# A hybrid decoder step: retention decay as factors, the causal mask added on TensorE, the ffn norm weights held in SBUF

## The chip, the cores and the metric

One of the eight cores of a Trainium2 chip runs the whole kernel; the others idle. The metric is the time of the kernel on the device in microseconds (us), the median of several executions.

## What is computed

One layer of a hybrid decoder in float32, for a prompt of 1024 tokens and for 8 sequences of 4 new tokens each (32 rows). The reference, cut to what matters here:

```python
def attend(q, k, v, q_pos, k_pos):                      # 8 heads of 96 (64 + 32 rotary)
    s = einsum('...qhd,...khd->...hqk', q, k) * 96 ** -0.5
    s = where(k_pos[None, :] <= q_pos[:, None], s, -inf)     # causal mask
    return einsum('...hqk,...khd->...qhd', softmax(s), v)

def retention_chunk(R, qkv):                            # chunks of 128 tokens, 8 heads of 64
    q, k, v = qkv
    lg = log1p(-2.0 ** (-5.0 - arange(8)))              # log decay of each head
    dmat = where(i >= j, exp(lg * (i - j)), 0.0)
    o = einsum('bhij,bjhv->bihv', einsum('bihd,bjhd->bhij', q, k) * dmat, v)
    o = o + einsum('bihd,bhdv->bihv', q, R) * exp(lg * (i + 1))
    R_new = exp(lg * 128) * R + einsum('bjhd,bjhv->bhdv', k * exp(lg * (127 - j)), v)
    return R_new, o

def peer_block(xb, ...):                                # 8 heads x 16 experts per token
    # queries against two sets of 128 keys, top 16 of each, top 16 of their 256 sums
    act = gelu(einsum('nd,nhkd->nhk', xb, peer_u[experts]))
    return einsum('nhk,nhkd->nd', softmax(vs) * act, peer_v[experts])

h = x + concat([mla_out, silu(rg) * group_norm(o)]) @ w_o
y = h + peer(rms_norm(h, ffn_norm_w))
```

The experts' tables `peer_u` and `peer_v` have 16384 rows of 1024 floats each. Every token gathers 128 rows of each.

## The kernel before

The program is written out engine by engine, with explicit semaphores. The prompt is cut into 8 tiles of 128 tokens (t = 0 to 7); the 32 new tokens are tile 8 ("the sample"), whose attention work is hung into tiles 1, 2 and 3.

**A tile's front** goes through these stages: projection of the normed x by ten weight pieces of 1 MB; latents, queries, keys, values and retention; attention of 8 heads over (t + 1) x 128 keys; the output projection (4 pieces); the residual and the ffn norm; the peer queries (8 pieces), the products with the two key sets, and the top-16 searches on VectorE that give the expert numbers (`codes`) and gates. Tiles 2, 4 and 6 are hosts: their input projection also does that of the next tile, the guest, so that tiles 3, 5 and 7 load no input weights. Tiles 2 and 3 also carry half of the sample's attention over paged caches.

**The expert stream** runs beside the front of the next tile. For each of a tile's 128 slots GpSimd (POOL) issues two indirect DMAs of 128 rows (512 KB): the u rows (`u_rows`, L805) into a ring of 8 buffers and the v rows (`v_rows`, L818) into a ring of 9. VectorE takes the dot of each u row with the token (`dot`, L1775, one multiply-and-reduce of 1024 columns). After 32 dots ScalarE applies the gelu (L1345) into `gelus`, VectorE multiplies by the gates into `coefs` and transposes (`make_coefs`, L1761), ScalarE spreads the coefficients into `Z` (L1361), and TensorE adds the v rows, weighted, into PSUM (`v_round`, L863). An object `Pace` holds a list of how many slots each engine does at each point of the front; on VectorE, TensorE and ScalarE the calls `slots()` do them in program order, between the front's own work. In attention, four slots stand beside each head in tiles 4 and 6, four or five in 5 and 7, and one or two in tiles 1 to 3.

**SP** issues all other DMAs, in one written order (`front`, L633; `load_tile`, L598; `load_piece`, L613). Two 1 MB buffers `wbuf` take the weight pieces in turn; in tile 0 the idle rings serve as eight more. A piece waits until the buffer's former piece is used. Since SP waits in order, each wait holds up all loads behind it.

**The table.** One buffer `table` of 128 x 1024 floats (L220) is used for three things in turn in every tile:
- the decay matrices `dec_in` of 8 heads (128 x 128 each), loaded by `load_tile` (L609) right after x and the rotary rows. `retention_decay` (L1950) multiplies the inner products by them (`inT`);
- the causal mask, (t + 1) x 128 columns, loaded by `load_mask` (L631) once the decay has been used. `attention` on VectorE (L1974) adds it to the scores of a head, taken from PSUM, and finds their maximum in the same instruction;
- the ffn norm weights, broadcast over partitions, loaded once all heads' scores are done (L666), in tiles 2 and 3 after the sample's scaled scores (L659). `norm_ffn` (L2000) multiplies by them. In those tiles `table` is also the scratch of a root (L400).

**Retention** in `qkv_and_retention` on TensorE (L1039): `retention_turn` transposes rq and rk (scaled by 0.125 in ScalarE's copy, L1516), `retention_inner` multiplies them, then come the cross products of q with the state R (L1060) and the new state's part kd x v (L1064), both signalled by `cross_ps`. `retention_out` (L1032) multiplies the decayed inner products by v (L1035). `heads_turn` (L1005) transposes queries and keys; it waits for `R_ready` of this tile, that is for VectorE's `retention_state` (L1955), which scales the cross products into `oret` (two halves), decays R and adds the new part. `retention_sum` (L1963) adds the inner part from PSUM. `heads_turn` is followed by the first scores (L1083), each signalled to VectorE by `scores_ps`; the next head's scores wait for `scores_ready`, since there is one score buffer in PSUM.

The constants (14 small loads, L763) are issued at the start between weight piece 1 and piece 2; VectorE waits for all of them in tile 0's `project`.

## Time and profile before

| what | us |
|---|---|
| median of 3 runs | 3536.87 |
| lowest and highest of them | 3530.06, 3540.1 |
| span of the profiled execution | 3534.4 |

The profiled execution is one of its own; the page gives its span, from the first to the last instruction, and no other time of it. PE is TensorE, PEld its weight loads, DVE VectorE, ACT ScalarE, POOL GpSimd, SP the engine that issues the plain DMAs (SPq its queue). A line is one of the kernel; L1745 and L1749 are the helpers through which most of VectorE's instructions pass, so those are told apart by the tiles they name. "x16" counts instructions; "[0.72 <-DVE nb]" is the idle time before an instruction and what ended it. "Issue" as a releaser means that the trace shows nothing the engine waited for. PEclk is TensorE's granted clock as a share of 2.4 GHz. The DMA share is the mean busy share of 16 DMA engines, GB/s what they moved.

### The profile page before, as it was taken

The numbers are of one execution on the slowest core, as the hardware profiler recorded it, in microseconds if no ns is written. First come the engines' busy times: TensorE is split into PE (matmuls) and PEld (weight loads), VectorE is DVE, ScalarE is ACT, GpSimd is POOL, SyncE is SP. The second block draws the span as 40 slices with busy tenths as digits, with TensorE's granted clock in tenths as the row PEclk, the third lists the DMA queues.
The fourth block names the chain that finished last, engine by engine and source line by source line (L and its number), as shares of the span: only waits on it lengthen the run. The fifth ranks groups of instructions, "written<-read, shape, count | busy, mean of one in ns | idle before, by whom it ended". The sixth has DMA issues, their size and how long they took to land.

```text
span 3534.4 us, 35434 instructions
## 1 busy us (share of the span) xinstructions
PE 2634.4 (75%) x11810; PEld 1284.3 (36%) x11810; DVE 2374.2 (67%) x6243; ACT 433.3 (12%) x980; POOL 2393.4 (68%) x2118
## 2 busy tenths in 40 slices
PE   6658676788867798797766777797877778767656
PEld 5634123553432344362232223463332234313211
DVE  4686667667678786767478765867478766847642
ACT  1101100113101231111001110111001110000000
POOL 0155776667757776657767777657767776677876
PEclk8879779898888989899889888999888999988799
DMA  6478999999999999999999999999999999999999
GB/s 252 169 277 313 367 349 408 352 397 369 366 404 362 380 348 408 407 400 377 380 411 402 388 377 409 395 412 395 381 410 397 396 399 407 397 408 384 322 410 371
DMA packets 372025, 1321.73 MB, mean 374 GB/s; under 512 B 60674, under 2 KB 72130, under 8 KB 351618
## 3 DMA queue, kind: packets, MB, share of 16 engines
q0 software_dynamic: 304128, 1107.43, 81.0%
q1 hardware_dynamic: 67714, 212.03, 15.4%
q8 instruction: 93, 1.52, 0.2%
q14 instruction: 90, 0.74, 0.1%
HBM read 1311.41 MB, written 7.88 MB: 373 GB/s over the span
## 4 chain that ended last, share of the span: by engine, by line
POOL 26%; PE 25%; DMA 22%; DVE 15%; issue 10%; SPq 2%; ACT 1%; DVEq 0%; POOLq 0%; ACTq 0%
POOL v_ring L818 13%; POOL u_ring L805 12%; DMA v_ring<-down_rows,codesT 12%; PE ps L863 8%; PE ps L927 6%; DMA u_ring<-up_rows,codes 6%; DMA wbuf<-weights 4%; DVE u_ring L1775 3%; DVE arena L1745 3%; PE ps L917 2%; PE ps L1127 2%; PE ps L1180 2%; DVE idx L1745 1%; DVE top_c L1745 1%; DVE top_v L1745 1%
## 5 line engine op out<-in xcount | busy, mean ns | idle before, releaser
L863 PE MATMUL ps<-v_ring,Z 128*32 128x512 f32 x4096 | 1324.0, 688 | 606.6 <-DMA v_ring<-down_rows,codesT 479.3
L1775 DVE CUSTOM_DVE_ANT_0 u_ring<-u_ring,xn 128x1024 f32<-128x1024 f32 x1056 | 1260.7, 1219 | 596.0 <-DMA u_ring<-up_rows,codes 595.5
L805 POOL DMA_INDIRECT u_ring<-up_rows,codes x1056 | 1191.4, 1128 | 676.6 <-issue 305.8
L818 POOL DMA_INDIRECT v_ring<-down_rows,codesT x1056 | 1200.8, 1137 | 449.3 <-issue 297.9
L863 PEld LDWEIGHTS ps<-v_ring,Z 128*32 128x32 f32 x4096 | 242.9, 118 | 1404.0 <-DMA v_ring<-down_rows,codesT 836.4
L927 PE MATMUL ps<-wbuf,xT 128*128 128x256 f32 (+2 forms) x1184 | 287.4, 401 | 64.8 <-DMA wbuf<-weights 36.5
L1127 PEld LDWEIGHTS ps<-xT,wbuf 128*128 128x128 f32 x2176 | 269.0, 202 | 160.8 <-issue 106.8
L1127 PE MATMUL ps<-xT,wbuf 128*128 128x128 f32 (+1 forms) x2176 | 292.1, 290 | 38.9 <-DMA wbuf<-weights 38.8
L927 PEld LDWEIGHTS ps<-wbuf,xT 128*128 128x128 f32 (+1 forms) x1184 | 226.8, 198 | 139.8 <-DMA wbuf<-weights 41.1
L1745 DVE MAX8 vals<-arena 128x8 f32<-128x128 f32 (+1 forms) x288 | 69.0, 280 | 113.9 <-ACT arena L1560 113.3
L917 PE MATMUL ps<-wbuf,kT 128*128 128x256 f32 (+1 forms) x480 | 104.7, 371 | 0.0
L1083 PE MATMUL ps<-kT,qT 96*128 96x512 f32 (+3 forms) x192 | 88.3, 573 | 15.7 <-DVE nb L1749 14.1
L1522 ACT ACTIVATE arena<-arena,nb 128x128 f32<-128x128 f32 (+7 forms) x64 | 49.6, 775 | 375.1 <-DVE nb L1749 375.1
L917 PEld LDWEIGHTS ps<-wbuf,kT 128*128 128x128 f32 x480 | 88.8, 190 | 11.2
L1775 DVE DVE_READ_ACCUMULATOR2_ANT dots<- 128x1 f32 x1056 | 86.6, 82 | 0.0
L1974 DVE CUSTOM_DVE_ANT_0 arena<-ps,table 128x128 f32<-128x128 f32 (+7 forms) x64 | 48.4, 756 | 51.3 <-PE ps L1083 42.2
L1745 DVE FIND_INDEX8 idx<-vals,arena 128x8 uint32<-128x128 f32 (+1 forms) x288 | 78.3, 283 | 0.0
L1560 ACT ACTIVATE arena<-ps 128x256 f32<-128x256 f32 (+1 forms) x72 | 27.4, 381 | 413.2 <-PE ps L1137 372.3
L1101 PEld LDWEIGHTS ps<-vN,arena 128*128 128x128 f32 x576 | 72.5, 198 | 6.2 <-issue 5.9
L1101 PE MATMUL ps<-vN,arena 128*128 128x64 f32 x576 | 74.7, 276 | 0.0
L1749 DVE TENSOR_REDUCE arena<-arena 128x8 f32<-128x512 f32 (+1 forms) x72 | 49.3, 684 | 37.0 <-ACT arena L1660 35.8
L1552 ACT ACTIVATE arena<-ps 128x256 f32<-128x256 f32 (+1 forms) x72 | 26.3, 366 | 370.7 <-PE ps L1127 370.7
(332 smaller groups left out, 2358.2 us busy)
## 6 DMA issues: line engine op xcount, KB each, us to landing
wbuf<-weights SPq DMA_DIRECT2D x142, 1024.0 KB, 8.3
u_ring<-up_rows,codes POOLq DMA_INDIRECT x1056, 8.6
v_ring<-down_rows,codesT POOLq DMA_INDIRECT x1056, 8.8
u_ring<-weights SPq DMA_DIRECT2D x8, 1024.0 KB, 14.7
v_ring<-weights SPq DMA_DIRECT2D x8, 1024.0 KB, 14.9
wbuf<-weights SPq DMA_DIRECT2D x9, 768.0 KB, 7.5
resid<-x_prompt SPq DMA_DIRECT2D x8, 512.0 KB, 7.0
table<-decay_in SPq DMA_DIRECT2D x8, 512.0 KB, 10.3
```

The costliest lines, as they stand in the source:

```text
L805: pool.indirect_dma_start(out=u_ring[:, i % U_RING, :], out_offset=None, in_=up_rows, in_offset=bass.IndirectOffsetOnAxis(ap=codes[:, t % ...
L818: pool.indirect_dma_start(out=v_ring[:, v % V_RING, :], out_offset=None, in_=down_rows, in_offset=bass.IndirectOffsetOnAxis(ap=codesT[:, t ...
L863: mm = pe.matmul(acc[32 * c:32 * c + 32, half, :], (Zs if t == TILES else Z)[:, at:at + GS], v_ring[:, v % V_RING, half * 512:(half + 1) * ...
L917: mm = pe.matmul(ps[:, 2 + S_BANK[w // 2], (w % 2) * PIECE:(w % 2) * PIECE + cols], xT_of(t + 1)[:, c], weights_of(t, w)[:, c, 0:cols], st ...
L927: mm = pe.matmul(out, xT[:, c, 0:n], weights_of(t, w)[:, c, 0:cols], start=(c == 0), stop=(c == DC - 1))
L1083: mm = pe.matmul(ps[:, 2 + c // 512, 0:e - c], qT[0:QK, s, :], kT[0:QK, s, c:e], start=True, stop=True)
L1101: mm = pe.matmul(ps[:, 6, h * 64:(h + 1) * 64], probT[:, h % 2, j * P:(j + 1) * P], vN[:, j, h * 64:(h + 1) * 64], start=(j == 0), stop=(j ...
L1127: mm = pe.matmul(ps[:, 4 + s % 2, j * P:j * P + n], weights_of(t, w)[:, c, j * P:(j + 1) * P], xT[:, c, 0:n], start=(c == 0), stop=(c == D ...
L1180: pe.matmul(ps[0:n, 6 + m % 2, :], lhs, uk, start=True, stop=True).then_inc(kn_ps, 1)
L1522: own.raises(act.activation(scores[:, s % 2, 0:w], scores[:, s % 2, 0:w], ACT.Exp, bias=nb[:, s:s + 1], scale=SCALE, accum_out=sums[:, s:s ...
L1745: own.done(instruction_of(*args, **kwargs))
L1775: dve.tensor_tensor_reduce(u, u, xn[:, t % 2], 1.0, 0.0, ALU.mult, ALU.add, dots[:, k:k + 1]).then_inc(dot_done, 1)
```

## The change

- The decay exp(lg (i - j)) is taken apart. The key side uses `kd` (k times exp(lg (127 - j)) / 8), which the state needs anyway: TensorE transposes kd in place of rk, and the inner products are only multiplied by a 0/1 triangle `upto` (128 x 128, broadcast over heads). The query side, exp(lg (i + 1 - 128)), is multiplied once on the sum of inner and cross part (`dec_out`).
- For that the state R is decayed first (in VectorE's `qkv`, from tile 1 on), and the cross products are accumulated into the same PSUM region as the inner ones, in `retention_out`. TensorE waits for `kd_ready` before `retention_turn`, and for `R_ready` (2t + 1) before `retention_out`; `heads_turn` waits for it no longer. VectorE scales the two halves from PSUM and adds the new part to R in `retention_sum`.
- The mask is added on TensorE: behind a head's scores, one product identity x `causal` (128 x 128) accumulates onto the last block. VectorE's instruction keeps its form; its second operand is a column of zeros, broadcast.
- The ffn weights lie in `ffn_wb`, loaded once; `causal`, `upto` and `ffn_wb` are three more constants. To make room, gelu and coefficients are written in place in `dots`; the root's scratch in tiles 2 and 3 becomes `lat`, `latn` and `th`, for which VectorE waits for the latents' store.
- All loads of `table` go, with SP's waits before them (`inner_ready`, `scores_ready`, `sT_ready`), and the order of the other loads stays.

```diff
...
         k2T = sb("k2T", [P, P])
-        dec_cross = sb("dec_cross", [P, H])
+        dec_out = sb("dec_out", [P, H])
+        causal = sb("causal", [P, P])
+        upto = sb("upto", [P, P])
+        none = causal[:, 0:1]
         dec_k = sb("dec_k", [P, H])
...
         rope_t = sb("rope_t", [P, 192])
-        table = sb("table", [P, D])
+        ffn_wb = sb("ffn_wb", [P, D])
         wbuf = sb("wbuf", [P, 2, DC, PIECE])
...
         kpw8 = arena[:, 3744:4000]
-        root_s = (table[:, 0:288], table[:, 288:576], table[:, 576:864])
+        root_s = (lat[:, 0:288], latn[:, 0:288], th[:, 0:288])
         mla_s = qflat[0:ST, 0:512]
...
                 sp.dma_start(rope_t[:], rope_rows[t * P:(t + 1) * P, :]).then_inc(tile_in, 16)
-                sp.dma_start(table[:], decay_in).then_inc(tile_in, 16)
...
                 sp.dma_start(pe, lat[0:n, QR + KVR:LAT]).then_inc(lat_stored, 16)
-
-            def load_mask(t):
-
-                sp.wait_ge(inner_ready, in_order(t) + 1)
-                sp.dma_start(table[:, 0:(t + 1) * P], mask_rows[:, (TILES - 1 - t) * P:TILES * P]).then_inc(mask_in, 16)
...
                 store_latents(t, lat_prompt[t * P:(t + 1) * P, :], pe_prompt[t * P:(t + 1) * P, :], P)
-                load_mask(t)
                 if t == S_TILE:
...
                 load_piece(t, O_0)
-                if t == B_TILES[0]:
-                    load_piece(t, O_0 + 1)
-                if t in B_TILES:
-                    sp.wait_ge(sT_ready, B_TILES.index(t) + 1)
-                    sp.dma_start(table[:], ffn_w.partition_broadcast(P)).then_inc(ffn_in, 16)
-                if t != B_TILES[0]:
-                    load_piece(t, O_0 + 1)
+                load_piece(t, O_0 + 1)
                 if t == S_TILE:
                     store_states()
-                if t not in B_TILES:
-                    sp.wait_ge(scores_ready, H * (t + 1))
-                    sp.dma_start(table[:], ffn_w.partition_broadcast(P)).then_inc(ffn_in, 16)
                 if t == B_TILES[-1]:
...
                              (q_wb, q_w.partition_broadcast(P)), (k_wb, k_w.partition_broadcast(P)),
-                             (ret_wb, ret_w.partition_broadcast(P)), (dec_cross, decay_cross), (dec_k, decay_k),
+                             (ret_wb, ret_w.partition_broadcast(P)), (dec_out, decay_out), (dec_k, decay_k),
                              (dec_state, decay_state), (k1T, keys1T), (k2T, keys2T), (ptab, page_table),
-                             (place_p, place_rows), (place_s, place_new), (spread, spread_new)):
+                             (place_p, place_rows), (place_s, place_new), (spread, spread_new),
+                             (causal, causal_rows), (upto, upto_rows), (ffn_wb, ffn_w.partition_broadcast(P))):
                 sp.dma_start(dst[:], src).then_inc(const_in, 16)
...
                 pe.wait_ge(inner_ready, in_order(t) + 1)
-                pe.wait_ge(R_ready, t + 2)
                 for h in range(H):
...
             def retention_turn(t, n, banks):
-                for src, b in zip((rq, rk), banks):
+                for src, b in zip((rq, of_s(t, rk, kd)), banks):
                     for r in range(4):
...
                 for h in range(H):
-                    mm = pe.matmul(ps[0:n, 3, h * 64:(h + 1) * 64], (inT if n == P else inT_s)[0:n, h, 0:n], rv[0:n, h * 64:(h + 1) * 64],
-                                   start=True, stop=True)
+                    a, at = 64 * (h % 2), 256 * (h % 2) + (h // 2) * 64
+                    out = ps[0:n, 3, h * 64:(h + 1) * 64] if t == TILES else ps[:, 3 + h % 2, at:at + 64]
+                    mm = pe.matmul(out, (inT if n == P else inT_s)[0:n, h, 0:n], rv[0:n, h * 64:(h + 1) * 64],
+                                   start=True, stop=(t == TILES))
+                    if t < TILES:
+                        mm = pe.matmul(out, rqT[a:a + 64, h // 2, :], R[a:a + 64, h // 2, :], start=False, stop=True)
                 mm.then_inc(o_ps, 1)
...
                 pe.wait_ge(rg_ready, in_order(t) + 1)
+                pe.wait_ge(kd_ready, t + 1)
                 retention_turn(t, P, (5, 0))
...
                 pe.wait_ge(v_ready, t + 1)
-                pe.wait_ge(R_ready, t + 1)
-                pe.wait_ge(kd_ready, t + 1)
                 for h in range(H):
                     a = 64 * (h % 2)
-                    pe.matmul(ps[:, 4 + h % 2, (h // 2) * 64:(h // 2 + 1) * 64], rqT[a:a + 64, h // 2, :], R[a:a + 64, h // 2, :],
-                              start=True, stop=True)
-                for h in range(H):
-                    a = 64 * (h % 2)
-                    mm = pe.matmul(ps[a:a + 64, 6, (h // 2) * 64:(h // 2 + 1) * 64], kd[:, h * 64:(h + 1) * 64],
+                    mm = pe.matmul(ps[a:a + 64, 4, (h // 2) * 64:(h // 2 + 1) * 64], kd[:, h * 64:(h + 1) * 64],
                                    rv[:, h * 64:(h + 1) * 64], start=True, stop=True)
-                mm.then_inc(cross_ps, 1)
-                slots()
+                mm.then_inc(state_ps, 1)
+                slots()
+                pe.wait_ge(R_ready, 2 * t + 1)
                 retention_out(t, P)
...
                         e = min(c + 512, (t + 1) * P)
-                        mm = pe.matmul(ps[:, 2 + c // 512, 0:e - c], qT[0:QK, s, :], kT[0:QK, s, c:e], start=True, stop=True)
+                        mm = pe.matmul(ps[:, 2 + c // 512, 0:e - c], qT[0:QK, s, :], kT[0:QK, s, c:e], start=True, stop=(e <= t * P))
+                    mm = pe.matmul(ps[:, 2 + t // 4, (t % 4) * P:(t % 4 + 1) * P], ident[:], causal[:], start=False, stop=True)
                     mm.then_inc(scores_ps, 1)
...
                 own.done(act.activation(rqT_[:, :, 0:n], src[0], ACT.Copy))
-                own.raises(act.activation(rkT_[:, :, 0:n], src[1], ACT.Copy, scale=0.125), rT_ready, in_order(t) + 1)
+                own.raises(act.activation(rkT_[:, :, 0:n], src[1], ACT.Copy, scale=of_s(t, 0.125, 1.0)), rT_ready, in_order(t) + 1)
...
                 do_signal(kd_ready, t + 1, dve.tensor_tensor, heads(kd), heads(rk[:]), over(dec_k[:], 2, [P, H, 64]), ALU.mult)
+                if t:
+                    do_signal(R_ready, 2 * t + 1, dve.tensor_tensor, R[:], R[:], over(dec_state[:], 2, [P, 4, 64]), ALU.mult)
                 slots()
...
                 dve.wait_ge(inner_ps, in_order(t) + 1)
-                do(dve.tensor_tensor, half(inT, 0), heads(bank(0), P), half(dec_in, 0), ALU.mult)
-                do_signal(inner_ready, in_order(t) + 1, dve.tensor_tensor, half(inT, 1), heads(bank(5), P), half(dec_in, 1), ALU.mult)
-
-            def retention_state(t):
-                dve.wait_ge(cross_ps, t + 1)
-                for a in range(2):
-                    do(dve.tensor_tensor, half(heads(oret), a), heads(bank(2 + a, P, 256)),
-                       over(dec_cross[:].rearrange("p (r a) -> p a r", a=2)[:, a], 2, [P, 4, 64]), ALU.mult)
-                do(dve.tensor_tensor, R[:], R[:], over(dec_state[:], 2, [P, 4, 64]), ALU.mult)
-                do_signal(R_ready, t + 2, dve.tensor_tensor, R[:], R[:], heads(bank(4, P, 256)), ALU.add)
+                do(dve.tensor_tensor, half(inT, 0), heads(bank(0), P), over(upto[:], 1, [P, 4, P]), ALU.mult)
+                do_signal(inner_ready, in_order(t) + 1, dve.tensor_tensor, half(inT, 1), heads(bank(5), P), over(upto[:], 1, [P, 4, P]), ALU.mult)
...
                 dve.wait_ge(o_ps, in_order(t) + 1)
-                do_signal(o_taken, in_order(t) + 1, dve.tensor_tensor, oret, bank(1), oret, ALU.add)
+                decay = dec_out[:].rearrange("p (r a) -> p a r", a=2)
+                do(dve.tensor_tensor, half(heads(oret), 0), heads(ps[:, 3, 0:256]), over(decay[:, 0], 2, [P, 4, 64]), ALU.mult)
+                do_signal(o_taken, in_order(t) + 1, dve.tensor_tensor, half(heads(oret), 1), heads(ps[:, 4, 256:512]), over(decay[:, 1], 2, [P, 4, 64]), ALU.mult, behind=1)
+                dve.wait_ge(state_ps, t + 1)
+                do_signal(R_ready, 2 * t + 2, dve.tensor_tensor, R[:], R[:], heads(bank(2, P, 256)), ALU.add)
             def attention(t, s):
-                if s == 0:
-                    dve.wait_ge(mask_in, 16 * (t + 1))
                 if s < H:
...
                     w = (t + 1) * P
-                    own.done(dve.tensor_tensor_reduce(scores[:, s % 2, 0:w], ps[:, 2:4, :].rearrange("p a b -> p (a b)")[:, 0:w], table[:, 0:w],
-                       1.0, LOWEST, ALU.add, ALU.max, mx[:, s:s + 1]))
+                    raw = ps[:, 2:4, :].rearrange("p a b -> p (a b)")[:, 0:w]
+                    own.done(dve.tensor_tensor_reduce(scores[:, s % 2, 0:w], raw, none[:, 0:1].to_broadcast([P, w]), 1.0, LOWEST, ALU.add, ALU.max, mx[:, s:s + 1]))
                     do_signal(scores_ready, H * t + s + 1, dve.tensor_scalar, nb[:, s:s + 1], mx[:, s:s + 1], -SCALE, None, ALU.mult)
...
                 root(n, 1)
-                dve.wait_ge(ffn_in, 16 * min(t + 1, TILES))
                 if t in HOSTS:
...
                 do_signal(wide_ready, wide_no(t, 2), dve.scalar_tensor_tensor, out=xn[0:n, t % 2], in0=resid[0:n],
-                          scalar=root_y[0:n, 0:1], in1=table[0:n], op0=ALU.mult, op1=ALU.mult)
+                          scalar=root_y[0:n, 0:1], in1=ffn_wb[0:n], op0=ALU.mult, op1=ALU.mult)
...
                 retention_decay(t)
-                retention_state(t)
                 slots()
...
                 new = ss_k[0:STEPS, :, 64:72]
+                dve.wait_ge(lat_stored, 32 * (in_order(B_TILES[i]) + 1))
                 do(dve.tensor_tensor, new, new, ss_new[0:STEPS, 32 * i:32 * i + 32].rearrange("p (b h) -> p b h", b=BATCH), ALU.add)
...
     out = dict(
-        rope_rows=rope_rows, rope_pages=rope_pages, mask_rows=mask_rows, mask_new=mask_new,
-        decay_in=inner(P).transpose(1, 0, 2), decay_cross=np.exp(lg[None] * (i[:, None] + 1)),
+        rope_rows=rope_rows, rope_pages=rope_pages, causal_rows=causal_rows, mask_new=mask_new,
+        upto_rows=(q <= c), decay_out=np.exp(lg[None] * (i[:, None] + 1 - P)),
         decay_k=np.exp(lg[None] * (P - 1 - i[:, None])) * f(0.125), decay_state=pairs(np.exp(lg * P)),
...
```

## Rows read from the trace of the kernel before

**Rows 1.** the page: span, POOL's busy time (share) and instructions, DMA traffic

```profile
span 3534.4 us, 35434 instructions
PE 2634.4 (75%) x11810; PEld 1284.3 (36%) x11810; DVE 2374.2 (67%) x6243; ACT 433.3 (12%) x980; POOL 2393.4 (68%) x2118
DMA packets 372025, 1321.73 MB, mean 374 GB/s; under 512 B 60674, under 2 KB 72130, under 8 KB 351618
```

**Rows 2.** stretches: length, PE PEld DVE ACT POOL busy, clock, DMA share, GB/s

```profile
20.00:60.00 40.00, 37.27 (x195) 31.53 (x193) 12.77 (x41) 7.25 (x18) 0.00 (x0) 1.00 1.00 416
60.00:120.00 60.00, 38.64 (x177) 31.79 (x176) 28.22 (x89) 9.24 (x30) 0.00 (x0) 0.68 0.04 14
1360.00:1560.00 200.00, 161.21 (x802) 100.26 (x799) 149.41 (x471) 24.36 (x57) 126.27 (x113) 0.92 1.02 408
1660.00:1760.00 100.00, 70.50 (x275) 29.97 (x276) 54.50 (x101) 7.63 (x20) 78.66 (x71) 0.90 0.99 372
2040.00:2100.00 60.00, 44.45 (x198) 19.26 (x196) 37.91 (x77) 6.49 (x15) 47.50 (x42) 0.93 0.98 366
2880.00:3080.00 200.00, 148.93 (x674) 68.45 (x674) 140.80 (x425) 16.64 (x37) 136.46 (x130) 0.92 1.02 409
```

**Rows 3.** timeline of VectorE and POOL: start, length, engine, line, operation [idle before]

```profile
1924.62 1.22 DVE L1775 CUSTOM_DVE_ANT_0 u_ring<-u_ring,xn 128x1024 f32<-128x1024 f32 x1
1924.65 1.99 POOL L818 DMA_INDIRECT v_ring<-down_rows,codesT  x1 [0.30 <-issue]
1926.95 0.94 POOL L805 DMA_INDIRECT u_ring<-up_rows,codes  x1 [0.30 <-issue]
```

**Rows 4.** POOL's waits over the run: us in total, times, longest

```profile
POOL u_ring L805 <- DVE codes L2043: 136.6, 1, 136.6
POOL u_ring L805 <- DVE dots L1775: 181.8, 55, 13.1
POOL v_ring L818 <- PE ps L863: 151.4, 141, 19.7
```

**Rows 5.** the page's DMA issues: KB each, median us to landing

```profile
table<-decay_in SPq DMA_DIRECT2D x8, 512.0 KB, 10.3
table<-ffn_w SPq DMA_DIRECT2D x8, 512.0 KB, 7.3
```

**Rows 6.** SP's timeline: one load each of decay, mask and ffn row

```profile
1373.15 0.43 SPq L609 DMA_DIRECT2D table<-decay_in  x1
1983.21 0.34 SPq L631 DMA_DIRECT2D table<-mask_rows  x1
2877.72 0.33 SPq L666 DMA_DIRECT2D table<-ffn_w  x1
```

**Rows 7.** a cycle with a guest and one without, columns as above

```profile
1372.00:1784.00 412.00, 320.01 (x1476) 169.78 (x1477) 270.99 (x710) 49.45 (x112) 286.36 (x258) 0.91 1.01 394
1784.00:2168.00 384.00, 277.43 (x1163) 113.69 (x1163) 266.38 (x682) 42.19 (x93) 285.29 (x255) 0.90 1.01 395
```

**Rows 8.** chain of waits at the end of tile 1: start, length, what

```profile
612.06 18.91 DMA wbuf<-weights
```

**Rows 9.** timeline of tile 0, before any expert row is gathered

```profile
6.78 1.06 ACT L1398 ACTIVATE arena<-resid 128x1024 f32<-128x1024 f32 x1 [4.74 <-DMA table<-decay_in]
59.77 0.98 PE L1060 MATMUL ps<-R,mix 64*128 64x64 f32 x14
68.34 3.67 PE L1035 MATMUL ps<-rv,xT 128*128 128x64 f32 x16 [6.54 <-DVE xT L1749]
89.24 0.79 PE L1083 MATMUL ps<-kT,qT 96*128 96x128 f32 x2 [0.53 <-DVE nb L1749]
138.51 1.09 POOL L805 DMA_INDIRECT u_ring<-up_rows,codes  x1 [136.63 <-DVE codes L2043]
```

**Rows 10.** VectorE's groups: busy us, mean ns, idle before

```profile
L1974 DVE CUSTOM_DVE_ANT_0 arena<-ps,table 128x128 f32<-128x128 f32 (+7 forms) x64 | 48.4, 756 | 51.3 <-PE ps L1083 42.2
L1745 DVE TENSOR_TENSOR mix<-ps,dec_cross 128x256 f32<-128x256 f32 x16 | 6.8, 425 | 2.9 <-PE ps L1064 2.0
```

More of the change, by code:

```diff
@@ L291, in hybrid_decoder_step @@
         dots = sb("dots", [P, SLOTS])
-        gelus = sb("gelus", [P, SLOTS])
-        coefs = sb("coefs", [P, SLOTS])
-        dec_in = table[:, :].rearrange("p (h i) -> p h i", h=H)
         def piece_of(t, w):
@@ L535, in hybrid_decoder_step @@
         s_oT = sem("s_oT")
-        N_CONST = 14
+        N_CONST = 17
         PROJECT = [3, 3, 4, 4, 3, 3]
@@ L1344, in gelu @@
                 at = slice(g * GS, (g + 1) * GS)
-                act.activation(gelus[:, at], dots[:, at], ACT.Gelu).then_inc(gelu_done, 1)
+                act.activation(dots[:, at], dots[:, at], ACT.Gelu).then_inc(gelu_done, 1)
             def make_Z(t, g):
@@ L1766, in make_coefs @@
                     dve.wait_ge(Z_ready, group_no(t, g) - 1)
-                do(dve.tensor_tensor, coefs[:, at], gelus[:, at], gates[:, t % 2, at], ALU.mult)
-                do_signal(coefT_done, group_no(t, g) + 1, dve.transpose, coefT[:, g % 2], coefs[:, at])
+                do(dve.tensor_tensor, dots[:, at], dots[:, at], gates[:, t % 2, at], ALU.mult)
+                do_signal(coefT_done, group_no(t, g) + 1, dve.transpose, coefT[:, g % 2], dots[:, at])
             def dot(t, k):
@@ L2382, in shape_constants @@
     rope_pages = rope(np.arange(PAGES * P), ROPE).reshape(PAGES, P, 64).transpose(1, 0, 2)
-    q, c = np.arange(P)[:, None], np.arange((2 * TILES - 1) * P)[None, :]
-    mask_rows = np.where(c - (TILES - 1) * P <= q, 0.0, -1e30).astype(f)
+    q, c = np.arange(P)[:, None], np.arange(P)[None, :]
+    causal_rows = np.where(c <= q, 0.0, -1e30).astype(f)
     mask_new = np.where(np.arange(STEPS)[None, :] <= (np.arange(P) % STEPS)[:, None], 0.0, -1e30).astype(f)
```

12 lines of the change are left out of this document (5 added, 7 removed).

## The prediction, made before the changed kernel was run

> **What bounds the kernel now.** The page comes first. The span is 3534.4 us, GpSimd (POOL) is busy for 68% of it and the DMA engines move 1321.73 MB [rows 1]. Neither figure says which of the two binds, so the table by stretches comes next [rows 2]. Two kinds of stretch alternate.
>
> In the first the transfers are at a ceiling. While tile 0's weights arrive and nothing else runs (20 to 60 us), 416 GB/s move. From 1360 to 1560 us (peer queries of tile 3, projections of tile 4) it is 408, from 2880 to 3080 us 409. In these stretches POOL has time left: one of its gathers is followed by 0.30 us in which it waits for nothing the trace shows [rows 3], so from 1360 to 1560 it is occupied for 126.27 + 113 x 0.30 = 160 of 200 us.
>
> In the second POOL itself is the bound. From 1660 to 1760 us, attention of tile 4, its occupation is 78.66 + 71 x 0.30 = 100.0 of 100 us; from 2040 to 2100, attention of tile 5, 47.50 + 42 x 0.30 = 60.1 of 60 us. The transfers then run at 372 and 366 GB/s: below what they did elsewhere, though the share column still says 0.98 and more. That column is thus no measure here; GB/s is. POOL is slow because a gather that starts under a VectorE dot lasts 1.99 us instead of 0.94 [rows 3].
>
> Between the two, POOL waits for room in the rings: 181.8 us for dots and 151.4 us for the v matmuls [rows 4]. Before all of it stands tile 0, a serial chain that ends with the first gather at 138.51 us, for which POOL waited 136.6 us [rows 4, 9]. What shortens or lengthens that chain moves the whole run.
>
> So a removed byte is worth 2.4 us per MB (1 MB / 410 GB/s) in a stretch at the ceiling, and nothing where POOL binds. A check: the cycle of tile 4, which also projects its guest, loads ten weight pieces of 1.05 MB more than the next cycle and lasts 412 instead of 384 us [rows 7]; 28 us for some 11 MB, 2.5 us per MB.
>
> **The transfers that go.** Per tile 1 to 7 the change drops a decay table of 512 KB, an ffn row of 512 KB [rows 5] and a mask of (t + 1) x 64 KB: 7 x 0.524 x 2 + 35 x 0.0655 = 9.63 MB. Tile 0's three are exchanged for constants of 0.66 MB.
> - Decay, tiles 4 to 7. It is issued at the start of the ceiling stretch (1373.15 us for tile 4, [rows 6]; the other three likewise, right behind the tile's x). Ahead of the weight pieces on SP's queue, it delays them: 0.524 MB / 410 GB/s = 1.28 us, times 4: **-5.1 us**.
> - Decay, tiles 2 and 3. Their stretch ends in a chain of page loads on SP, in which TensorE then waits for a piece issued only at 612.06 us [rows 8]. There the issue alone counts, 0.43 us by [rows 6]: I take 0.5 each, **-1.0 us** (bounds 0 and 2.6). Decay of tile 1 is loaded with the machine nearly idle: 0.
> - Masks. That of tile 5 is issued at 1983.21 us [rows 6], inside attention, where POOL binds before and after: 0, as for the six others. Cover: POOL's full occupation. Were it gone, 2.29 MB would be 5.6 us.
> - The ffn row. Same place, 0, except in tile 7: issued at 2877.72 us [rows 6], with a stretch at 409 GB/s behind it [rows 2]: **-1.3 us**. Bound with the cover gone: 7 x 1.28 = 9.0 us.
> Sum -7.4 us; with everything priced, 9.63 MB / 410 GB/s = -23.5 us.
>
> **The waits that go.** SP no longer waits for the inner product, the end of the scores, or sT before it goes on to the output weights. The first two output pieces of a tile start some tens of us earlier; the next two need buffers that only the output projection frees, so nothing later moves. TensorE needs them only after attention: 0. If they crowd out gathers, the same 2.1 MB is merely moved. VectorE waits for neither mask nor ffn row; the trace names neither as something it waited for: 0. In tiles 2 and 3 it waits for the latents' store before it uses their buffers as scratch; that store was issued long before attention: 0, and nothing is queued behind it that waits now.
>
> **Retention.** VectorE loses one of seven products per tile (two of 425 ns [rows 10] and a 512-column sum become two products from PSUM): about -0.7 us a tile, beside POOL's bound in tiles 1 to 7: 0. TensorE turns kd instead of rk, so it waits for one more VectorE product (0.7 us); in tile 0 it arrives later than that anyway, elsewhere v rounds cover it; uncovered it is 0.7 us a tile. The heads' transposes no longer wait for the state update, which was done in time in tile 0: 0. But the cross products (16 instructions) move behind the inner ones, onto the path. Fourteen took 0.98 us at full clock [rows 9], so 16 take 1.1 us, and 2.2 us at the 0.68 of this stretch or below [rows 2]: tile 0 **+1.6 us** (the middle). The masks by broadcast operands cost nothing: the product with a broadcast operand has the pace of a plain one (425 ns for 256 columns [rows 10]). The state decay moves ahead by some 15 us on VectorE; 0.4 us, absent in tile 0.
>
> **The mask on TensorE.** No row shows the added product (identity times a 128x128 block, two instructions). Nearest is L1035, also 128x128 weights: 3.67 / 16 = 0.229 us each, at reduced clock [rows 9]; 0.46 us per head. Bounds: 0 if it hides, 0.46. In tile 0 a head goes round in 1.38 us, scores (0.79 us [rows 9]), maximum, bias, scores. Heads 1 to 4 have group norm work on VectorE behind them, which hides the addition for heads 2, 3, 4; five heads remain: 5 x 0.46 = **+2.3 us**. In tiles 4 to 7 four expert slots, eight gathers of 1.4 us = 11 us, lie beside each head; 0.46 us vanishes.
>
> **The start.** ScalarE waited until 6.78 us for the decay table [rows 9]; now x and the rope rows suffice, issued 0.5 us earlier with 0.52 MB less in flight: **-1.0 us** (bounds 0 and -1.5). Three constants are issued ahead of piece 2, about 1.5 us net; the pieces arrived without a wait of TensorE before; 0, at worst +1.
>
> **Sum** against the profiled execution: -7.4 + 1.6 + 2.3 - 1.0 = -4.5 us, a span of 3529.9. The median of the runs is 3536.87, 2.5 us above that span; the same step from it gives **3532.4 us**.
>
> **The rivals.**
> 1. *Transfers bind everywhere.* For it: the cycles of [rows 7] both move about 395 GB/s, and the share column is near 1. Against: POOL's full occupation at 372 and 366 GB/s. Then 23.5 us go, less 2.9 for tile 0: 3516.3.
> 2. *The stretches at 366 to 372 GB/s are themselves the ceiling.* Then a MB there costs 2.7 us, 9.63 MB 26 us; less 2.9: 3513.8. Rows at 408 to 416 GB/s in the same kernel speak against it. The Trainium skill, "DMA: Bandwidth & Descriptors", section "Where 436 GB/s comes from", puts the limit of HBM to SBUF traffic of one core at about 358 GB/s; by it the gain would be 26.9 us before tile 0's cost. By that rule no stretch here could pass 358, and the trace disagrees with 416.
> 3. *Slower: the score chain of tiles 1 to 3 becomes the bound.* There a head has one or two slots beside it (2.8 us of gathers), and VectorE already waited 42.2 us for score products [rows 10]. From the point where a head's round passes its gathers, each of 24 heads adds 0.46 us: +11.0, with tile 0's 2.9 and no gain from bytes, 3550.8. Against it: POOL is hardly ever starved in attention.
> 4. *The bytes were hidden wholly,* because VectorE's top-k or TensorE's projections, over 0.7 busy in ceiling stretches, set their length: only tile 0's +2.9 is left, 3539.8.
>
> **How the numbers follow.** Forecast 0.54, rival 1 0.22, rival 2 0.04, rival 3 0.10, rival 4 0.10. The range reaches from rival 1 with a little room, 3515, to rival 4 with a few us for the open price of the mask, 3544; it leaves out rivals 2 and 3 and some edges. A measurement of this kernel can tell about 0.3%, 10.6 us, from no change. Faster by more: rivals 1 and 2 and an edge of the forecast (the masks' and ffn rows' cover partly gone), 0.33. Slower by more: most of rival 3, 0.07. Within: 0.60.
>
> **What the profile of after would show.** First gather near 141.4 us instead of 138.5; POOL still at full occupation in attention at 365 to 380 GB/s; tiles 4 to 7 each about 1.3 us shorter; TensorE some 20 us busier. If attention stretches get faster by several us each, rival 1 holds. If VectorE's wait for L1083 grows by over 10 us and POOL's wait for dots with it, rival 3 does. I would be wrong most simply if the chance overlaps of dots and gathers shift: they decide between 0.94 and 1.99 us for each gather, and no row tells which way they fall.

## The result: 0.4% slower, and the profile after

The kernel after takes 3549.36 us (median of 10 runs, 3542.41 to 3564.74) beside 3534.99 us for the kernel before (10 runs, 3530.06 to 3545.84): **1.0037 times the time, 95% interval 1.0021 to 1.0053**. 4.5 us less was forecast; some 13 us more is what came, beyond the range (3515 to 3544). Profiles differ by 10.9 us (3545.3 against 3534.4).

The page of the kernel after, the lines that answer to [rows 1]:

```profile
span 3545.3 us, 35664 instructions
PE 2691.7 (76%) x11938; PEld 1339.7 (38%) x11938; DVE 2368.3 (67%) x6234; ACT 433.1 (12%) x980; POOL 2393.2 (68%) x2118
DMA packets 369002, 1311.65 MB, mean 370 GB/s; under 512 B 60338, under 2 KB 71666, under 8 KB 348594
```

10.1 MB are gone, as the diff says (9.63 MB of tiles 1 to 7, and 0.46 net in tile 0). TensorE is 57 us busier, where 20 were forecast. VectorE's timeline in tile 0 of the kernel before, to read beside [rows 9]:

```profile
68.39 0.88 DVE L1745 TENSOR_TENSOR mix<-ps,dec_cross 128x256 f32<-128x256 f32 x2
69.30 0.42 DVE L1745 TENSOR_TENSOR R<-R,dec_state 128x256 f32<-128x256 f32 x1
69.76 0.42 DVE L1749 TENSOR_TENSOR R<-R,ps 128x256 f32<-128x256 f32 x1
72.05 0.69 DVE L1749 TENSOR_TENSOR mix<-ps,mix 128x512 f32<-128x512 f32 x1 [1.87 <-PE ps L1035]
```

Tile 0 in the kernel after, PE, DVE and POOL:

```profile
22.99 9.33 PE L910 MATMUL ps<-u_ring,xT 128*128 128x256 f32 x42 [1.88 <-DMA u_ring<-weights]
...
68.83 0.66 PE L1019 MATMUL ps<-rv,xT 128*128 128x64 f32 x2 [6.58 <-DVE xT L1732]
69.42 0.69 PE L1022 MATMUL ps<-R,mix 64*128 64x64 f32 x2
70.03 0.69 PE L1019 MATMUL ps<-rv,xT 128*128 128x64 f32 x2
70.65 0.69 PE L1022 MATMUL ps<-R,mix 64*128 64x64 f32 x2
...
78.05 0.69 PE L1022 MATMUL ps<-R,mix 64*128 64x64 f32 x2
78.67 1.94 PE L992 MATMUL ps<-ident,arena 128*96 128x128 f32 x8
...
78.77 0.42 DVE L1728 TENSOR_TENSOR mix<-ps,dec_out 128x256 f32<-128x256 f32 x1 [10.09 <-PE ps L1022]
...
147.09 1.09 POOL L788 DMA_INDIRECT u_ring<-up_rows,codes  x1 [145.21 <-DVE codes L2021]
```

Retention's output, 3.67 us before [rows 9], is now followed by the next product 9.84 us after its start (68.83 to 78.67): one head after the other, an inner product (128 rows of the contraction) and a cross product (64 rows) start 0.617 us apart. The granted clock is 0.50 in this stretch, as it was from 68.3 to 72 us in the kernel before, so the clock isn't the difference. VectorE stands idle for 10.09 us where it had 1.87, since the work that it did under the inner products before is gone from that place. The first gather starts 8.6 us later. What the earlier start gained (2.0 us at ScalarE's first operation) is gone by the second projection piece, for which TensorE waits 1.88 us in this profile.

Over the whole run, VectorE's waits (us in total, times, longest), first that for retention's output in the kernel before, then those of the kernel after:

```profile
DVE mix L1749 <- PE ps L1035: 1.9, 1, 1.9
```

```profile
DVE u_ring L1758 <- DMA u_ring<-up_rows,codes: 562.8, 350, 8.5
DVE mix L1728 <- PE ps L1022: 51.3, 8, 10.1
DVE arena L1954 <- PE ps L1066: 38.3, 29, 3.7
```

and TensorE's groups, shapes apart (busy us, mean ns):

```profile
L1022 PE MATMUL ps<-R,mix 64*128 64x64 f32 x128 | 36.7, 379 | 0.0
L1019 PE MATMUL ps<-rv,xT 128*128 128x64 f32 x128 | 35.9, 373 | 13.7 <-DVE xT L1732 13.7
L1066 PE MATMUL ps<-causal,ident 128*128 128x128 f32 x128 | 26.2, 287 | 0.0
```

The second wait of the kernel after is the new one, once in each of the eight tiles: 51.3 us instead of 1.9. The wait for the scores, which rival 3 lives on, fell: 38.3 us against 42.2 [rows 10]. The mask product takes 26.2 us of TensorE, and yet VectorE's wait for the scores, which now ends with that product, didn't grow.

One difference between the profiles is no effect of the change. From the sample's load on (2957.9 us) to the end the kernel after takes 587.4 us against 579.0 before. But kernels whose code there is that of before took 584.9, 584.4 and 588.0 us for the same stretch (the three with a delay, below). Differences of a few us between two profiles in the time of a long stretch are therefore not read as effects below.

### The profile page after: what moved, and what is told of

Same layout as the page of the kernel before. It is cut to its first block, busy times and chain, and to the rows that moved or that the text cites. A ratio compares the mean times of both kernels' runs of the same rounds, so it can differ in the third digit from the quotient of the medians.

```text
span 3545.3 us, 35664 instructions
## 1 busy us (share of the span) xinstructions
PE 2691.7 (76%) x11938; PEld 1339.7 (38%) x11938; DVE 2368.3 (67%) x6234; ACT 433.1 (12%) x980; POOL 2393.2 (68%) x2118
## 4 chain that ended last, share of the span: by engine, by line
POOL 28%; PE 26%; DMA 18%; DVE 15%; issue 11%; SPq 2%; ACT 1%; DVEq 0%; POOLq 0%; ACTq 0%
POOL v_ring L801 14%; POOL u_ring L788 14%; DMA v_ring<-down_rows,codesT 9%; PE ps L846 8%; PE ps L910 6%; DMA u_ring<-up_rows,codes 5%; DMA wbuf<-weights 4%; DVE u_ring L1758 3%; DVE arena L1728 3%; PE ps L900 2%; PE ps L1110 2%; PE ps L1163 2%; DVE idx L1728 1%; DVE top_c L1728 1%; DVE top_v L1728 1%
## 5 line engine op out<-in xcount | busy, mean ns | idle before, releaser
L1728 DVE FIND_INDEX8 idx<-vals,arena 128x8 uint32<-128x128 f32 (+1 forms) x288 | 78.3, 283 | 0.0
L1954 DVE CUSTOM_DVE_ANT_0 arena<-ps,causal 128x128 f32<-128x128 f32 (+7 forms) x64 | 48.4, 756 | 39.3 <-PE ps L1066 38.3
```

The lines of the kernel that those rows point to most:

```text
L1728: own.done(instruction_of(*args, **kwargs))
```

## The experiments

All ratios are to the kernel before run on the same chip. "Early" below is the second kernel.

**1. Products grouped.**

```
-for h: inner(h); cross(h)
+for h: inner(h)
+for h: cross(h)
```

> The kernel after, with the eight inner products of retention issued first and the eight cross products behind them, the same 16 matmuls into the same PSUM regions, so that a 128-row product no longer alternates with a 64-row one. Theory A (the alternation is what made tile 0's retention output 9.9 us long instead of 3.67 us plus about 1 to 1.6 us): it takes 5 to 5.5 us in tile 0 and 3 to 3.7 us at full clock in the other tiles (5.8 now), the first gather starts at 142 to 143 us instead of 147.1, and the time falls by 3 to 6 us from the kernel after (3543 to 3546). Rival B (each accumulation onto a just written region costs its time wherever it stands): tile 0 stays near 9.9 us, the first gather at 147, the time at 3549.

The edit also leaves the start flag (`start=True` in the kernel's call) on the first product of each PSUM bank alone.

Measured: **0.9986 (0.9968 to 1.0005)**, 3531.44 us; from 1.0037 that is 0.0051 +- 0.0025, 18 +- 9 us. PE in its tile 0:

```profile
66.26 3.65 PE L1020 MATMUL ps<-rv,xT 128*128 128x64 f32 x16 [7.25 <-DVE xT L1741]
69.83 1.97 PE L1025 MATMUL ps<-R,mix 64*128 64x64 f32 x16
71.74 1.94 PE L992 MATMUL ps<-ident,arena 128*96 128x128 f32 x8
```

The same sixteen products take 5.48 us instead of 9.84, at the same granted clock (0.50). In tiles 1 to 7 they take 3.9, 5.5 and five times 3.0 us, where the kernel after has 9.4, 9.3, 5.9, 6.1, 8.0, 7.7 and 7.8. Theory A holds, and gave too small a time: it counted tile 0 and little more. The first gather starts at 141.48 us, but not all of the 5.6 us come from the order: in this profile retention's output already begins 2.6 us sooner (66.26 against 68.83), by code that is the same.

**2. Cross products early.** They go behind the state products, while VectorE still prepares heads; the inner ones accumulate onto them (the start flag stands on the first product of each PSUM bank alone).

```
 mm.then_inc(state_ps, 1)
+pe.wait_ge(R_ready, 2 * t + 1)
+for h: matmul(out(h), rqT(h), R(h), start=(h < 2), stop=False)
 slots()
-pe.wait_ge(R_ready, 2 * t + 1)
```

> The kernel after, with the cross products of retention issued right behind the state products, before the inner products' wait, which they open; the inner products then accumulate onto them. The wait for the state moves with them. Theory A (what was mis-sized is the retention output on tile 0's chain): only the eight inner products are left there, 3.7 us instead of 9.9, first gather at 140.5 to 141.5 us, and the time falls by 5 to 8 us, to 3541 to 3545. If the delay of tile 0 doesn't reach the end (Rival C: the later tiles' phase of dots and gathers sets what is lost), the first gather moves all the same and the time stays within 3 us of 3549.

> The kernel with the cross products moved ahead once more, unchanged, beside the next run and on the same chip. Expected: 0.9956 of the kernel before within 0.002.

Measured: **0.9956 (0.9934 to 0.9978)** and **0.9965 (0.9946 to 0.9984)**, 3520.34 and 3525.27 us; mean 0.9961 +- 0.0015. That is 27 us below the kernel after, 9 +- 8 below the grouped one, and faster than the kernel before. That is far more than the 5 to 8 us expected. Tile 0 of the first of the two, first gather at 139.39 us:

```profile
58.73 1.97 PE L1049 MATMUL ps<-R,mix 64*128 64x64 f32 x16
66.60 3.67 PE L1019 MATMUL ps<-rv,xT 128*128 128x64 f32 x16 [5.90 <-DVE xT L1734]
```

VectorE's wait for retention's output, grouped (first line) and early (second):

```profile
DVE mix L1737 <- PE ps L1025: 18.0, 6, 5.7
```

```profile
DVE mix L1730 <- PE ps L1019: 8.5, 6, 3.8
```

51.3, 18.0, 8.5: this wait falls by 33.3 and 9.5 us, the time by about 18 and 9. The profiles also say where the time arrives. Retention's output starts in the kernel after, beside the two runs of the early one, 8 us later in tile 1 (331.39 against 323.35 and 323.06), 20 and 22 in tile 4 (1620.38 against 1600.81 and 1598.46), 26 and 28 in tile 7 (2783.32 against 2757.48 and 2755.43). Most of the loss is made before tile 5, though the output takes some 6 us more in tiles 5 to 7 too.

**3. Why alternation costs: shifted, and in pairs.** Two kernels with one execution each, so only their timelines are read. The first puts cross h-2 behind inner h, the second goes inner, inner, cross, cross.

> The kernel after, with the cross product of head h-2 behind the inner product of head h: 128-row and 64-row products still alternate, but no product accumulates onto the one just issued. Theory A1 (the change between 128 and 64 rows, from one product to the next, is what costs): tile 0's retention output takes 8.5 to 9.9 us as in the kernel after. Theory A2 (the accumulation onto the region just written costs): 5.5 to 6 us as with the products grouped.

> The kernel after, with retention's products in fours: inner h, inner h+1, cross h, cross h+1. 7 changes of the row count where the kernel after has 15 and the grouped one 1. If each change costs the same (9.9 us with 15, 5.5 us with 1: 0.31 us each at the half clock): 7.2 to 7.6 us in tile 0. If it is instead that two products with different rows next to each other never overlap while the second of a pair does, the same; if the cost is of the cross product behind an inner one alone: 6.5 to 7. If it is the number of PSUM groups opened: 9.9.

PE in tile 0 of the shifted kernel:

```profile
68.72 0.69 PE L1025 MATMUL ps<-R,mix 64*128 64x64 f32 x2
69.34 0.69 PE L1020 MATMUL ps<-rv,xT 128*128 128x64 f32 x2
69.95 0.69 PE L1025 MATMUL ps<-R,mix 64*128 64x64 f32 x2
```

The step is the same 0.61 us though nothing accumulates onto what was just written; the whole takes 8.65 us (67.28 to 75.93). So A1: it is the change between 128 and 64 rows. The start flags stand here as in the grouped kernel, so they aren't what made that one fast. In pairs:

```profile
69.21 1.09 PE L1020 MATMUL ps<-rv,xT 128*128 128x64 f32 x4 [6.61 <-DVE xT L1742]
70.23 0.69 PE L1025 MATMUL ps<-R,mix 64*128 64x64 f32 x4
70.86 1.11 PE L1020 MATMUL ps<-rv,xT 128*128 128x64 f32 x4
```

A four takes 1.65 us, all eight pairs 6.65: less than the 7.2 to 7.6 of a fixed cost per change. Two cross products side by side (rows 0 to 63 and 64 to 127) take 0.63 us together, as one does alone when a 128-row product stands on either side. Read so, the alternation loses twice: at each change (two inner products take 1.02 us here and 0.89 in a block), and by the overlap of the two halves, which a lone cross product doesn't have. The division between the two is an argument from these steps, not a run of its own. The Trainium skill says of both, in "TensorEngine Tiling (Array Packing)", section "Key Properties", that changing the tiling mode drains TensorE, and that different tiles run in parallel. The trace agrees, with 0.617 us a step against 0.446 (inner) and 0.24 (cross) when grouped, all at a granted clock of 0.50.

**4. Mask product left out**, from the kernel after and, twice, from the early one.

```
-mm = pe.matmul(ps[diagonal block], ident[:], causal[:], start=False, stop=True)
```

> The kernel after, leaving out the causal mask product (the output is then attention without a causal mask in the diagonal block). Theory D (the mask product is a large part of the loss, through tile 0's eight rounds and the score chain of the others): first gather near 144 us, time down by 6 us or more. Theory A: the eight rounds of tile 0 shrink by 0.42 us for each of five to seven of them, first gather at 144 to 145 us, and the time falls by 2 to 3.5 us, to 3546 to 3547.5; tiles 1 to 3 no shorter than now.

> Unchanged, the kernel with the cross products moved ahead, leaving out the causal mask product (no causal mask in the diagonal block). The mask product is the rest of the sum: 0.9940 or lower of the kernel before. 2.3 us or none: 0.9950 to 0.9965.

Without it, attention has no causal mask in its diagonal block. Measured: 1.0029 (1.0014 to 1.0045) against 1.0037 with it; 0.9957 (0.9938 to 0.9976) against 0.9961: 3 and 1 us, each +- 8, not to be told from nothing. The medians neither confirm nor refute the forecast's 2.3 us; together they exclude a price of 10 us or more. (The first's profile has its first gather at 149.6 us, its retention output having begun 2 us later.)

The timelines of tile 0 say more. The last two score products of the kernel before, then of the kernel after:

```profile
89.24 0.79 PE L1083 MATMUL ps<-kT,qT 96*128 96x128 f32 x2 [0.53 <-DVE nb L1749]
90.62 0.79 PE L1083 MATMUL ps<-kT,qT 96*128 96x128 f32 x2
```

```profile
96.69 0.80 PE L1065 MATMUL ps<-kT,qT 96*128 96x128 f32 x2 [0.33 <-DVE nb L1732]
98.49 0.80 PE L1065 MATMUL ps<-kT,qT 96*128 96x128 f32 x2
```

This round grew from 1.38 to 1.80 us. But the rounds of 2.08 to 3.78 us in the middle didn't grow, and from the first score product to the eighth it is 14.58 us in the kernel after (83.91 to 98.49) and 15.09 in the early one (74.63 to 89.72), against 14.13 before (76.49 to 90.62).

**5. Does a longer chain reach the end?** The kernel before with its eight inner products issued three times over, in tile 0, in tiles 1 to 3, in tiles 4 to 7.

```
-for h in range(H):
+for h in list(range(H)) * (3 if t == 0 else 1):      # or 1 <= t < 4, or 4 <= t < TILES
```

> The kernel before, with the eight inner products of tile 0 issued three times over (the same values, written again), 7.3 us more on tile 0's chain and nothing else changed. If a delay of tile 0 passes to the end whole (Theory A for the size of the loss): first gather at 145.8 us and the time up by 6 to 8.5 us, to 3541 to 3543.5. Rival C (the delay is taken up again where transfers are ahead, or the phase of dots and gathers that it shifts decides): up by under 3 us, or by more than 10.

> The kernel before, with the eight inner products of retention issued three times over in tiles 1 to 3: 2 x 2.7 us more on TensorE between the decay and the heads' turn in each, 16.3 us in all. Theory E (in every tile VectorE waits for retention's output with nothing else ready, so what lengthens that chain reaches the time): up by 8 to 16 us, to 3544 to 3552 where the kernel before is at 3536. Theory of the prediction (the chain binds in tile 0; in tiles 1 to 3 the ring's dots fill the wait): up by under 4 us.

> The kernel before, with the same tripling in tiles 4 to 7 alone: 2 x 2.7 us more in each, 21.8 us in all, and nothing in tiles 0 to 3. Theory of the prediction (in these tiles the transfers run at 395 to 410 GB/s and bind, so a longer chain on TensorE is covered): up by under 4 us. Theory E: up by 10 to 20 us, to 3546 to 3556; the transfers were then not what bound the tile, but the chain through VectorE.

Measured: 1.0012 (0.9998 to 1.0026), 1.0021 (1.0005 to 1.0038), 1.0010 (0.9994 to 1.0027): +4, +7 and +4 us, each +- 5 to 6. By the traces, 6.8, 19.5 and 14.3 us were added to TensorE's output products, not quite what was expected for the last two (16.3 and 21.8): from tile 3 on the eight take 2.00 us once and 5.57 three times over. VectorE's wait in the first and the last:

```profile
DVE mix L1749 <- PE ps L1035: 10.5, 3, 8.7
```

```profile
DVE mix L1749 <- PE ps L1035: 9.2, 3, 4.1
```

Of 6.8 us more in tile 0 (10.50 against 3.67), some 4 arrive. In tiles 4 to 7 some 4 of 14.3 do, and VectorE waits only 7 us more there. The answer lies between the theories: of 41 us added in all three, 15 +- 10 reach the time. For a single group of tiles the intervals are too wide to say more; that the late tiles absorb the most fits the lag by tiles in 2. A part of the same order, 18 +- 9, arrives of the 34 us by which grouping shortens these products.

**6. Bytes and SP's wait put back** into the early kernel, apart and together.

```
+if t: sp.dma_start(ffn_wb[:], ffn_w.partition_broadcast(P))     # twice a tile, 7.34 MB
```
```
+sp.wait_ge(inner_ready, in_order(t) + 1)
 load_piece(t, O_0)
```

> The kernel with the cross products moved ahead (the edit of the second run), and the ffn weights loaded again twice per tile in tiles 1 to 7 (512 KB at the place of the decay table, 512 KB behind the latents' stores where the mask was loaded, each waited for before the ffn norm): 7.34 MB more, no other work. The kernel without these loads stood 15.7 us under the kernel before. Theory of the prediction (bytes count in tiles 4 to 7 alone): 4 x 1.05 MB at 410 GB/s, 10.2 us, plus about 1 us in tiles 2 and 3: 3531 if the kernel before is at 3536. Bytes count everywhere: 7.34 MB at 410 GB/s, 17.9 us, 3538. Bytes hidden: within 3 us of 3520. What the loads cost is then also what most of the 15.7 us came from, or isn't.

> The kernel with the cross products moved ahead, and SP waiting for the inner products of retention before it loads the first output piece, as it did for the mask. No byte and no operation more. Expected by the prediction, which priced this at nothing: within 3 us of the kernel without the wait (0.9956 of the kernel before). Rival (the queue no longer held up is part of the gain): 5 us or more above that.

> The kernel with SP's wait for the inner products put back, once more, unchanged. If the wait is worth what the first comparison gave (0.9986 against 0.9956, some 10 us): 0.9980 or above. If that was scatter of the medians: within 0.0015 of the run beside it.

> Unchanged, both the loads and SP's wait put back into the kernel with the cross products moved ahead. Additive: 1.002 to 1.004 of the kernel before. One gain: 0.999 to 1.000.

Measured: bytes 0.9990 (0.9971 to 1.0009); wait 0.9986 (0.9968 to 1.0003) and 0.9997 (0.9977 to 1.0018); both 1.0005 (0.9989 to 1.0021). Against 0.9961: bytes +10 +- 8 us, wait +11 +- 7, both +16 +- 8. At the forecast's prices (2.4 us per MB in tiles 4 to 7) these loads cost 11 us, and the bytes agree with that. The second of them isn't at the old mask's place, though: without SP's wait it goes out at 1579.43 us in tile 4, in a stretch of 406 GB/s. The wait doesn't agree: it was priced at nothing. Only the wait for `inner_ready` was put back; those for the end of the scores and for sT were not tested.

SP's timeline around tile 4's output pieces, early kernel, then with the wait:

```profile
1566.15 0.63 SPq L623 DMA_DIRECT2D pe_prompt<-lat  x1
1569.19 183.08 SPq L618 DMA_DIRECT2D wbuf<-weights  x6
```

```profile
1566.78 0.68 SPq L623 DMA_DIRECT2D pe_prompt<-lat  x1
1595.87 164.25 SPq L618 DMA_DIRECT2D wbuf<-weights  x6
```

Without the wait the first two pieces start 26 us sooner after the latents' store. Why that pays is open. It isn't that POOL has time left there: from 1569 to 1600 us of the early kernel its occupation is 24.32 + 22 x 0.30 = 30.9 of 31 us. The transfers run at 407 GB/s in that stretch (413 in the repeat), and at 352 between store and pieces in the kernel with the wait (394 in its repeat, 361 in the kernel before); that the wait leaves room unused which is missing later would fit, but isn't shown. Whether bytes and wait add could not be told: 16 lies between one gain alone and 21.

**7. Constants later.** In the early kernel, the causal block and the upto block are loaded behind the projection pieces of tile 0, the ffn row behind its output pieces.

> The kernel with the cross products moved ahead, and the three new constants loaded behind the projection pieces of tile 0 (causal and upto) and behind its output pieces (ffn weights) instead of ahead of all ring pieces. Expected: the second projection piece starts at 21 us instead of 23.0, the first gather near 137.4 to 138 us instead of 139.4, and the time 1 to 3 us lower (0.995 of the kernel before), which the measurement can hardly tell. Rival (the start doesn't matter since transfers of 512 KB pieces pace the projections of tile 0 anyway): the queries of tile 0 start no earlier, same time.

Measured: 0.9957 (0.9940 to 0.9975), 3524.88 us. The second piece doesn't wait (PE, start of tile 0):

```profile
20.38 11.82 PE L914 MATMUL ps<-u_ring,xT 128*128 128x256 f32 x54
```

and the time is that of the early kernel. The profile alone can't say that moving the constants did this: with the constants in their old place the second piece started at 20.85 us in the early kernel and at 20.41 in the grouped one, without a wait either. Over the 15 profiles of kernels with the three constants ahead of it, TensorE's wait for it is 0 in two and 0.3 to 3.7 us in thirteen; in the five profiles without them (before, the three with a delay, this one) there is none.

**Without an answer.** Both put back, no mask in the early kernel, and the kernel after with SP's wait ran once more beside a kernel before that took 3711 us: 0.9982 (0.9948 to 1.0015), 0.9990 (0.9957 to 1.0024), 1.0020 (0.9988 to 1.0052). In that set every kernel was some 170 us slower, with transfers at 355 GB/s on the page instead of 370, and its intervals don't separate terms of 10 us. What the last of them was to tell stays open; for the other two it hangs on the repeats in 4 and 6:

> The kernel with the cross products moved ahead, with both the 7.34 MB of loads put back and SP's wait put back. If the two gains add (12 and 10 us as measured apart): 1.002 to 1.004 of the kernel before, 3543 to 3550, and the 7 to 12 us that this stands above the kernel before are then what the mask product and the other edits cost. If the two are one gain (the wait only hurts where it holds transfers back that later bind): 0.999 to 1.000.

> The kernel with the cross products moved ahead, leaving out the causal mask product (no causal mask in the diagonal block). If the mask product is what is left of the sum: 0.9940 or lower of the kernel before, 6 us or more below the kernel with it (0.9956 and 0.9965). As the prediction has it (2.3 us, in tile 0 alone): 0.9950 to 0.9960, which can hardly be told from none.

> The kernel after itself, with SP's wait for the inner products put back ahead of the first output piece. If the wait is worth 10 us here too: 1.0055 to 1.0075 of the kernel before (3555 to 3562). As the prediction has it (nothing): 1.0037 within 0.0015.

## Why the prediction was wrong

The account, from the ratios above:

```
bytes and SP's wait, taken away together        -16 +- 8 us
everything else but the cross products' place    +2 +- 6   (2.3 MB less among it)
cross products on the path, grouped              +9 +- 8
and alternating with the inner ones             +18 +- 9
sum                                             +13   (measured +13)
```

The last line is no independent check, since the terms are differences of one chain of kernels.

- **"Tile 0 +1.6 us" for retention is the step that failed**, in size and in reach. It added 16 cross products at the pace that they have among themselves, [rows 9], to inner ones at theirs. For a block that price is right: grouped, the output takes 5.54 us instead of 3.67, 1.9 more. In the diff they alternate, and at that pace (0.617 us each) it takes 9.91 us (68.83 to 78.74): +6.2 in tile 0. And the forecast stopped at tile 0. The forecast wrote that VectorE's saved product lies "beside POOL's bound in tiles 1 to 7: 0" and took the same for TensorE's addition. But before, VectorE scaled the cross products and updated the state under the inner ones (68.39 to 70.18 us in tile 0); the change moved that cover behind them. Its wait rose from 1.9 to 51.3 us over eight tiles, and the time by 27 us against the early kernel, where the cross products are off the path.
- **"The waits that go ... 0"**: the second failure, of the other sign: 11 +- 7 us gained by the wait for `inner_ready` alone. "Nothing later moves" was nearly true of SP's queue (the next two pieces of tile 4 are issued at 1732.11 and 1746.27 us in the early kernel, at 1734.89 and 1747.02 with the wait) and false of the time.
- **Transfers -7.4**: measured -10 +- 8 for 7.34 MB, as much as seven decay tables and seven ffn rows. In reach. The mechanism (dear at the ceiling, free elsewhere) isn't shown; rival 1's price for these bytes, 17.9 us, lies just inside the interval, and so isn't refuted. One reading under it was wrong: the masks aren't loaded inside attention. Tile 5's is issued at 1983.21 us, 3 us before retention's output, and from 1983 to 2010 us 402 GB/s move while POOL is occupied for 21.21 + 20 x 0.30 = 27.2 of 27 us. The forecast's two kinds of stretch overlap there, and its price of 0 has no clean ground.
- **Mask +2.3**: too large by the timeline. Where a head's round grew, it was by 0.42 us (1.38 to 1.80), where 0.46 was priced; but that held for one round of the kernel after and two of the early one, not for five heads. The seven rounds of tile 0 grew by 0.45 and 0.96 us together. Rival 3 is out as a cause: the wait for scores fell, and leaving the product out gained 3 and 1 us, each +- 8, where its 11 in tiles 1 to 3 and the 2.3 of tile 0 should have shown.
- **Start -1.0**: ScalarE began 2.0 us earlier, all of it lost again by piece 2, which starts 0.3 us later than before. "0, at worst +1" for the three constants was too mild: TensorE's wait behind them is 0 to 3.7 us from one profile to the next (7). Without them ahead the time was no shorter.
- **Rival 3's time**, 3550.8 us, came within 1.4 of the result. That is luck: its mechanism, the score chain, is the one that the waits and the kernels without the mask speak against. **Rival 4** (bytes hidden wholly, 3539.8) lies just below what was measured for bytes, 2 to 18 us. **Rival 2** took 366 to 372 GB/s for a ceiling; the traces exclude it, since with POOL at full occupation 402 and 407 GB/s move in the kernel before (1983 to 2010, 2010 to 2040 us).
- First gather: 141.4 forecast, 147.09 measured; grouped and early 141.48 and 139.39. That 141.48 is the forecast to 0.1 us is luck, since retention's output begins anywhere from 66.1 to 72.9 us in kernels with the new start. From that output's start to the first gather it is 70.2 us before, 78.3 after, 75.2 grouped, 72.8 and 72.5 early.
- Of the other signs, POOL was at full occupation in attention at 372 and 368 GB/s (1670 to 1770 and 2046 to 2106 us), as forecast. That "the chance overlaps of dots and gathers" had a part in the loss is shown by no run; the order of sixteen products accounts for most of it.

That the loss could come from the products' alternation was in none of the rivals: all four asked what binds, and none whether an added instruction keeps the pace of the row that it was priced from.

## What to carry to other kernels

Price an added TensorE product (a matmul) by the neighbours that it will have, not by a row of its own kind in a block: group products by their row count, and put the 64-row ones of both halves side by side. When work is moved behind a wait, look at what the waiting engine did meanwhile; that cover moves too. A factored decay, fewer loads and no queue wait were worth 0.4% here (0.9961 of the time before), once sixteen small products stood in the right place.

## What the hardware showed beyond expectation

- TensorE at the 1.2 GHz level: 0.617 us for each product of an alternating sequence of 128-row and 64-row products (64 columns, f32, two instructions each), 0.446 and 0.24 us in blocks of one kind. The granted clock is 0.50 in all these stretches (68.8 to 78.7 us after, 66.2 to 71.8 grouped). In tile 3, where it is 1.00, the alternating sixteen take 5.89 us and the grouped ones 3.03.
- Transfers at 402 to 409 GB/s and a fully occupied POOL go together in the same stretch (1983 to 2010 and 1630 to 1660 us of the kernel before).
- Runs of one kernel of this length scatter by 0.4% (3538.51 to 3552.55, 12 runs with the delay in tiles 1 to 3) to 0.9% (3515.79 to 3546.64, 12 runs of the early kernel with SP's wait), so that 12 runs beside some 30 of the kernel before leave +- 6 us, and two profiles can differ by 9 us in a stretch whose code is the same.
- The kernel before took 3535 to 3538 us (medians) in five sets of runs and 3711 us in one, with 355 GB/s in its companions' profiles.
